# A two-layer transformer with a modulated second block: three modulation weight units loaded one up unit later

## The chip, the core and the metric

The kernel runs on one core of a Trainium2 chip. Five engines work from their own instruction streams: TensorE (matrix products, into the banks of PSUM), VectorE, ScalarE, GpSimd and SyncE, which here only issues loads from the memory of the chip (HBM) into SBUF, the on-chip memory of 128 partitions. Streams wait for one another with semaphores. The metric is the device time of one execution in microseconds (us); all tensors are 32-bit floats.

## The reference

Two blocks work on 256 tokens of 1024 features. The first has two layers, each a mixer (convolution, differential attention and memory attention side by side) and a feed-forward part; the second has one layer whose norms are scaled, shifted and gated by six vectors that are one product of a condition vector `c` with a 1024 x 6144 weight. The change touches the feed-forward part of the two layers and the place of that product:

```python
for l in range(2):                                   # first block
    x = layer_norm(ALPHA * x + hybrid_mixer(x, ...), ln1_g[l], ln1_b[l])
    ff = square(relu(x @ w_up[l])) @ w_down[l]        # 1024 -> 4096 -> 1024
    x = layer_norm(ALPHA * x + ff, ln2_g[l], ln2_b[l])
...
mod = silu(c) @ ada_w + ada_b                         # second block: 6 vectors of 1024
shift_m, scale_m, gate_m, shift_f, scale_f, gate_f = split(mod, 6)
```

## The kernel before

**Units.** Weights are read in units of 1024 x 512 (2 MB) into `ring`, three slots of SBUF in turn (`RING`, line 34). A layer has 30 units (`layer_units`, line 62): one for the memory, five for the mixer's input, two for its output, then the feed-forward part: eight of `w_up` and eight of `w_down`, called units 0 to 7 and 8 to 15 here, and six of `ada_w`, the modulation units 0 to 5. `ADA_UP` and `ADA_DOWN` (line 39) say behind which up and down units the modulation units lie, three and three in each layer. The whole modulation product, twelve units, is made in this way beside the feed-forward parts of the two layers. Everything else about the order follows from these two tuples: `ADA_AT` holds the positions of the modulation units in the order of loading, `ADA_POSITIONS` the steps in which they are worked on.

**SyncE** issues the loads in the order of the list. Before each it waits for its slot (`slot_free`, line 466): until TensorE is through with the unit three places earlier (seen at the first products of the unit behind it), or, if that was a modulation unit, until VectorE has summed it. A load whose slot is not free holds up all loads behind it.

**An up or down unit** is one step of Winograd's form of the 2 x 2 block product: seven products on TensorE instead of eight, in the order m1, m3, m2, m6, m5, m7, m4 (`seven`, line 2375; unit 0 opens with m1, m2, m4). m1, m2, m3 and m7 take blocks of the loaded weights; m5, m6 and m4 take sums of such blocks. VectorE makes these sums (`weight_sums`, line 1346): four operations on 128 x 1024 elements, of which m5 needs the first, m7 the second, m6 the third, m4 the fourth. They go by turns to tiles in `mid` and in `work`, so m6 of a unit reads in a row of the timeline as `acc<-ysq,mid` or `acc<-ysq,work`, m1 as the first `acc<-x,ring` of its unit. In step u, with TensorE on unit u, VectorE does, in this order:

```python
if u in ADA_POSITIONS:
    ada_sums(ADA_POSITIONS.index(u))        # L1572
if u + 1 < FFN_UNITS:
    weight_sums(u + 1)
if u - 2 in ADA_POSITIONS:
    ada_columns(ADA_POSITIONS.index(u - 2)) # L1576
...
    combine(u)                              # up units: the seven products put together
```

**A modulation unit** is not multiplied on TensorE. ScalarE scales its eight rows of blocks by silu(c) (`ada_scale`, line 898, eight operations), VectorE adds the eight to one row (`ada_sums`, line 1288, three operations of 2048, 1024 and 512 columns), TensorE turns the row into columns (`ada_turned`, four 128 x 128 turns, behind the unit after), and VectorE reduces these (`ada_columns`).

**ScalarE**, in step g, first makes the hidden group g - 1 from VectorE's combination (`hidden`: two relus at line 893, one square at 896), then copies the first bank of unit g (`first_bank`, line 887), then scales a modulation unit:

```python
hidden(g - 1)
first_bank(g)
if g + 1 in ADA_UP:
    ada_scale(ADA_UP.index(g + 1))
```

**GpSimd** makes the sums of tokens that the down units need, in quarters q: four operations on 128 x 512 elements (lines 582 to 587) as soon as the hidden groups 2q and 2q + 1 are there; quarters 2 and 3 wait besides until TensorE is through with units 9 and 11.

Of the kernel before, what the change touches and what calls it, by code (L numbers as in the profile page):

```python
# [35 lines left out]
UCOLS = 512  # L36
UROWS = 8
LAYER_UNITS = 30
ADA_UP, ADA_DOWN = (1, 3, 5), (0, 2, 4)
LAYER_ACCS = 20  # L40
HEAD_SIDE = (1, 0, 1)
OUT_BANKS = (2, 3, 0, 1)
# [3134 lines left out]
```

## Time and profile before

| what | value |
|---|---|
| median of 3 runs | 1304.3 us (1304.15 to 1304.51) |
| the profiled execution | 1303.27 us, of which the span from first to last instruction is 1301.3 |
| TensorE busy | 1287.2 us, 99% of the span |
| VectorE busy | 940.2 us, 72% |
| ScalarE busy | 423.2 us, 33% |
| GpSimd busy | 178.2 us, 14% |
| granted TensorE clock | 0.998 of full speed |
| feed-forward units, layer 0 and 1 | from 138 to 339 us, from 464 to 664 us |

The views name the engines PE (TensorE), DVE (VectorE), ACT (ScalarE), POOL (GpSimd) and SP (SyncE). A row of the timeline gives the start in us from the beginning of the span, the time to the end of the last of the operations that are merged in it, the engine, the line of the kernel, the operation, output<-inputs, shape and number; in square brackets, where the engine had been idle, the idle time and what ended it. Matmuls overlap one another a little, so the distance of two starts is the better measure of a product than its length. A releaser is the semaphore event that came last.

### The profile page before, as it was taken

The numbers are of one execution on the slowest core, as the hardware profiler recorded it, in microseconds if no ns is written. First come the engines' busy times: TensorE is split into PE (matmuls) and PEld (weight loads), VectorE is DVE, ScalarE is ACT, GpSimd is POOL, SyncE is SP. The second block draws the span as 40 slices with busy tenths as digits, with TensorE's granted clock in tenths as the row PEclk, the third lists the DMA queues.
The fourth block names the chain that finished last, engine by engine and source line by source line (L and its number), as shares of the span: only waits on it lengthen the run. The fifth ranks groups of instructions, "written<-read, shape, count | busy, mean of one in ns | idle before, by whom it ended". The sixth has DMA issues, their size and how long they took to land.

```text
span 1301.3 us, 34012 instructions
## 1 busy us (share of the span) xinstructions
PE 1287.2 (99%) x15139; PEld 1145.2 (88%) x15139; DVE 940.2 (72%) x1603; ACT 423.2 (33%) x920; POOL 178.2 (14%) x164
## 2 busy tenths in 40 slices
PE   9999999999999999999999999999999999999997
PEld 7975899988898589998877889999999986999986
DVE  4985798656698479867782789998997845765753
ACT  2254334311225433432144424555742103110101
POOL 3100322021000042203125010003100100011200
PEclk9999999999999999999999999999999999999999
DMA  9632567577443256757738797335645544654540
GB/s 330 200 130 97 195 226 284 199 267 256 142 151 130 98 195 231 283 201 266 249 93 231 179 251 205 131 131 185 207 131 196 191 168 130 196 170 157 179 178 33
DMA packets 132930, 243.17 MB, mean 187 GB/s; under 512 B 7237, under 2 KB 37725, under 8 KB 132273
## 3 DMA queue, kind: packets, MB, share of 16 engines
q1 hardware_dynamic: 122506, 218.00, 48.7%
q0 software_dynamic: 9872, 22.80, 7.2%
q8 instruction: 120, 1.97, 0.6%
q10 hardware_dynamic: 407, 0.20, 0.1%
q14 instruction: 25, 0.20, 0.0%
HBM read 231.49 MB, written 6.34 MB: 183 GB/s over the span
## 4 chain that ended last, share of the span: by engine, by line
PE 88%; DVE 7%; DMA 2%; issue 1%; ACT 1%; POOL 1%; SPq 0%; DVEq 0%
PE acc L2214 55%; PE scr L2214 17%; PE pvw L2214 9%; DVE mid L1523 2%; PE scr L2824 1%; PE scr L2319 1%; DMA ring<-in_w_mem_kv 1%; PE ptb L2214 1%; PE ptb L2328 1%; DMA ring<-in_w_up 1%; PE pvw L2338 1%; PE pvw L2858 1%; PE ptb L2658 0%; DMA strip_rows<-hid 0%; DVE hid L1882 0%
## 5 line engine op out<-in xcount | busy, mean ns | idle before, releaser
L2214 PE MATMUL acc<-y,ring 128*64 128x128 f32 (+1 forms) x2048 | 154.1, 283 | 0.0
L2214 PEld LDWEIGHTS acc<-y,ring 128*64 128x64 f32 (+1 forms) x2048 | 139.3, 142 | 8.5 <-issue 2.3
L2214 PE MATMUL acc<-ring,big 128*128 128x256 f32 (+1 forms) x376 | 115.6, 454 | 0.0
L2214 PEld LDWEIGHTS acc<-ring,big 128*128 128x128 f32 x376 | 70.6, 190 | 33.4 <-issue 27.0
L2214 PE MATMUL acc<-ring,hid 128*128 128x256 f32 (+1 forms) x364 | 99.1, 417 | 0.0
L2214 PE MATMUL acc<-x,ring 128*64 128x128 f32 (+1 forms) x1472 | 98.9, 278 | 0.0
L2214 PEld LDWEIGHTS acc<-x,ring 128*64 128x64 f32 (+1 forms) x1472 | 89.6, 139 | 4.7 <-issue 3.2
L903 ACT ACTIVATE ring<-ring,silc 128x512 f32<-128x512 f32 x96 | 60.1, 709 | 93.8 <-DMA ring<-in_ada_w 93.8
L2214 PEld LDWEIGHTS acc<-ring,hid 128*128 128x128 f32 x364 | 68.4, 190 | 22.2 <-issue 14.9
L2214 PE MATMUL acc<-ysq,ring 128*64 128x128 f32 x1184 | 71.2, 273 | 0.0
L1295 DVE TENSOR_TENSOR ring<-ring 128x2048 f32<-128x2048 f32 (+1 forms) x24 | 44.2, 1843 | 33.7 <-ACT ring L903 33.2
L2214 PE MATMUL scr<-ysq,ring 128*64 128x128 f32 x1120 | 67.5, 273 | 0.0
L2214 PEld LDWEIGHTS acc<-ysq,ring 128*64 128x64 f32 x1184 | 66.4, 137 | 0.0
L2214 PEld LDWEIGHTS scr<-ysq,ring 128*64 128x64 f32 x1120 | 62.8, 137 | 0.0
L1523 DVE SCALAR_TENSOR_TENSOR mid<-upad,pc,mid 128x256 f32<-128x256 f32 x120 | 48.7, 476 | 0.0
L728 ACT ACTIVATE work<-work,nm 128x256 f32<-128x256 f32 x80 | 39.6, 496 | 25.8 <-DVE nm L1269 15.6
L1146 ACT ACTIVATE big<-acc 128x512 f32<-128x512 f32 x19 | 11.3, 596 | 109.7 <-PE acc L2214 109.7
L1354 DVE TENSOR_TENSOR mid<-ring 128x1024 f32<-128x1024 f32 x16 | 19.5, 1221 | 36.7 <-DMA ring<-in_w_down 24.2
L1355 DVE TENSOR_TENSOR ring<-ring 128x1024 f32<-128x1024 f32 x32 | 45.4, 1420 | 0.0
L582 POOL TENSOR_TENSOR big<-hid 128x512 f32<-128x512 f32 x8 | 15.1, 1884 | 212.6 <-PE pvw L2214 150.4
L2214 PE MATMUL acc<-mid,ring 128*64 128x128 f32 x704 | 41.0, 273 | 0.0
L893 ACT ACTIVATE hid<-big 128x512 f32<-128x512 f32 x16 | 10.1, 629 | 90.7 <-DVE pt L1399 90.6
(592 smaller groups left out, 2771.8 us busy)
## 6 DMA issues: line engine op xcount, KB each, us to landing
ring<-in_w_in SPq DMA_DIRECT2D x24, 2048.0 KB, 10.9
ring<-in_w_up SPq DMA_DIRECT2D x16, 2048.0 KB, 8.7
ring<-in_w_down SPq DMA_DIRECT2D x16, 2048.0 KB, 7.9
ring<-in_ada_w SPq DMA_DIRECT2D x12, 2048.0 KB, 12.9
ring<-in_w_ffn_in SPq DMA_DIRECT2D x22, 1024.0 KB, 7.1
ring<-in_w_out SPq DMA_DIRECT2D x6, 2048.0 KB, 7.9
ring<-in_w_o_ssd SPq DMA_DIRECT2D x4, 2048.0 KB, 8.5
ring<-in_w_ffn_out SPq DMA_DIRECT2D x4, 2048.0 KB, 8.3
```

The source lines that it names most:

```text
L582: pool.tensor_tensor(s1, a21, a22, ALU.add).then_inc(sh_ready, 1)
L728: ins = act.activation(pr[:, i % 2, j, :], lg[:, i % 2, j, :], ACT.Exp, scale=-1.0, bias=nm[:, i % 2, j:j + 1], accum_out=zz[:, i % 2, j:j ...
L903: act.activation(ring[:, n % RING, k, :], ring[:, n % RING, k, :], ACT.Copy, scale=silc[:, 1, k:k + 1]).then_inc(ada_scaled, 1)
L1295: steps.link(tt(w[:, 0:width, :], w[:, 0:width, :], w[:, width:2 * width, :], ALU.add))
L1354: tt(t[:, 0], b12, b11, ALU.subtract).then_inc(t_ready, 1)
L1355: tt(b12, b22, b12, ALU.subtract).then_inc(t_ready, 1)
L1523: ins = stt(cy[:, c, :], upad[:, c, tap:tap + T], w, cy[:, c, :], ALU.mult, ALU.add)
L2214: ins = pe.matmul(dst, w, m, start=start, stop=stop, is_transpose=turned, skip_group_check=True)
L2319: ins = pe.matmul(scr[m][:, t, :], q[half, t * P:(t + 1) * P], keys[half, h, :], start=True, stop=True)
L2328: ins = pe.transpose(ptb[:, 2 * j + kt, :], at[:, i % 2, j, kt * P:(kt + 1) * P], ident[:, :])
L2338: ins = pe.matmul(pvb[:, 0, :], vt[:, h * P:(h + 1) * P], pt[:, i % 2, kt, :], start=kt == 0, stop=kt == TT - 1)
L2824: ins = pe.matmul(scr[i % 2][:, m, :], q2[:, 2 * j + m, t * P:(t + 1) * P], kvn[:, :], start=True, stop=True)
```

## The change

One tuple of three numbers changes:

```diff
--- before.py
+++ after.py
@@ -36,7 +36,7 @@
 UCOLS = 512
 UROWS = 8
 LAYER_UNITS = 30
-ADA_UP, ADA_DOWN = (1, 3, 5), (0, 2, 4)
+ADA_UP, ADA_DOWN = (2, 4, 6), (0, 2, 4)
 LAYER_ACCS = 20
 HEAD_SIDE = (1, 0, 1)
 OUT_BANKS = (2, 3, 0, 1)
```

The first three modulation units of each layer are loaded behind up units 2, 4 and 6 instead of 1, 3 and 5, and what is done with them moves one step on each engine. On SyncE, at the beginning and at the end of the up units of a layer (`ring<-in_w_up` an up unit, `in_ada_w` a modulation unit, `in_w_out` the mixer's output, `in_w_down` a down unit):

```order
 L482 DMA ring<-in_w_out 128x8x512 x2
-L482 DMA ring<-in_w_up 128x8x512 x2
+L482 DMA ring<-in_w_up 128x8x512 x3
 L482 DMA ring<-in_ada_w 128x8x512
 L482 DMA ring<-in_w_up 128x8x512 x2
```

```order
 L482 DMA ring<-in_ada_w 128x8x512
-L482 DMA ring<-in_w_up 128x8x512 x2
+L482 DMA ring<-in_w_up 128x8x512
 L482 DMA ring<-in_w_down 128x8x512
 L482 DMA ring<-in_ada_w 128x8x512
```

Three up units come before the first modulation unit, and one instead of two lies between the third modulation unit and the first down unit. The slots change with the places: modulation units 0, 1 and 2 followed one another in the slot that the mixer's last unit left, and it went on to the first down unit; now they follow one another in the slot that unit 0 leaves, which goes on to modulation unit 3, and the first down unit takes the slot of unit 6.

On VectorE, from the end of combination 1 (line 1399) on; lines 1295 and 1296 are a modulation sum, lines 1354 to 1359 the weight sums of one unit, the combination follows at line 1388. Before:

```order
L1399 TENSOR_TENSOR pt<-big,pvw 128x256
L1354 TENSOR_TENSOR work<-ring 128x1024
L1355 TENSOR_TENSOR ring<-ring 128x4x256
L1357 TENSOR_TENSOR work<-ring,work 128x1024
L1359 TENSOR_TENSOR work<-ring,work 128x1024
L1388 TENSOR_TENSOR big<-pt,acc 128x512
```

Now:

```order
L1399 TENSOR_TENSOR pt<-big,pvw 128x256
L1295 TENSOR_TENSOR ring<-ring 128x2048
L1295 TENSOR_TENSOR ring<-ring 128x1024
L1296 TENSOR_TENSOR pre<-ring 128x512
L1354 TENSOR_TENSOR work<-ring 128x1024
L1355 TENSOR_TENSOR ring<-ring 128x4x256
L1357 TENSOR_TENSOR work<-ring,work 128x1024
L1359 TENSOR_TENSOR work<-ring,work 128x1024
L1388 TENSOR_TENSOR big<-pt,acc 128x512
```

The modulation sum 0 has moved from step 1 to step 2, where it stands ahead of the weight sums of unit 3; steps 4 and 6 get the next two in the same way, and steps 1, 3 and 5 lose theirs.

On ScalarE, at the beginning of the up units (line 887 the copy of a first bank, 903 the scaling, 893 and 896 a hidden group):

```order
 L887 ACTIVATE pt<-acc 128x512
+L893 ACTIVATE hid<-big 128x4x128
+L893 ACTIVATE hid<-pt 128x4x128
+L896 ACTIVATE hid<-hid 128x1024
+L887 ACTIVATE pt<-acc 128x512
 L903 ACTIVATE ring<-ring,silc 128x512 x8
```

The first scaling stands behind hidden group 0 and the bank of unit 1, and so ahead of hidden group 1; it used to stand ahead of hidden group 0.

## Rows read from the trace of the kernel before

**Rows 1.** Page, part 4: the chain that ended last, by engine.

```profile
PE 88%; DVE 7%; DMA 2%; issue 1%; ACT 1%; POOL 1%; SPq 0%; DVEq 0%
```

**Rows 2.** Timeline, unit 2: start us, us, engine, operation [idle before].

```profile
164.76 1.95 PE L2214 MATMUL acc<-x,ring 128*64 128x128 f32 x32
...
168.25 1.95 PE L2214 MATMUL acc<-x,ring 128*64 128x128 f32 x32
170.49 1.97 PE L2214 MATMUL acc<-ysq,mid 128*64 128x128 f32 x32 [0.29 <-DVE mid L1357]
...
495.45 1.95 PE L2214 MATMUL acc<-ysq,mid 128*64 128x128 f32 x32
...
165.03 0.58 ACT L887 ACTIVATE pt<-acc 128x512 f32<-128x512 f32 x1
```

**Rows 3.** Timeline, TensorE: first products of units 4 to 6, m6 of 5.

```profile
190.49 1.92 PE L2214 MATMUL acc<-x,ring 128*64 128x128 f32 x32
...
203.41 1.97 PE L2214 MATMUL acc<-x,ring 128*64 128x128 f32 x32
...
208.70 1.92 PE L2214 MATMUL acc<-ysq,work 128*64 128x128 f32 x32
...
215.68 1.92 PE L2214 MATMUL acc<-x,ring 128*64 128x128 f32 x32
```

**Rows 4.** Timeline, ScalarE and SyncE's queue: scalings 1 and 2, unit 6's load.

```profile
179.27 5.01 ACT L903 ACTIVATE ring<-ring,silc 128x512 f32<-128x512 f32 x8 [2.37 <-DMA ring<-in_ada_w]
...
205.29 5.01 ACT L903 ACTIVATE ring<-ring,silc 128x512 f32<-128x512 f32 x8 [6.17 <-DMA ring<-in_ada_w]
...
203.87 12.59 SPq L482 DMA_DIRECT2D ring<-in_w_up  x2
```

**Rows 5.** Timeline, VectorE, layer 0: modulation sum 0, weight sums, combination 1.

```profile
162.76 3.54 DVE L1295 TENSOR_TENSOR ring<-ring 128x2048 f32<-128x2048 f32 x2
...
166.95 1.22 DVE L1354 TENSOR_TENSOR mid<-ring 128x1024 f32<-128x1024 f32 x1
...
169.22 1.22 DVE L1357 TENSOR_TENSOR mid<-ring,mid 128x1024 f32<-128x1024 f32 x1
...
171.61 0.68 DVE L1388 TENSOR_TENSOR big<-pt,acc 128x512 f32<-128x512 f32 x1
...
174.05 1.22 DVE L1354 TENSOR_TENSOR work<-ring 128x1024 f32<-128x1024 f32 x1
```

**Rows 6.** Timeline, three engines: quarter 1's sums, layer 0; modulation sum 4, layer 1.

```profile
196.40 0.63 ACT L893 ACTIVATE hid<-big 128x512 f32<-128x512 f32 x1 [9.50 <-DVE pt L1399]
...
198.72 1.27 POOL L582 TENSOR_TENSOR big<-hid 128x512 f32<-128x512 f32 x1 [15.16 <-ACT hid L896]
...
201.16 2.29 DVE L1355 TENSOR_TENSOR ring<-ring 128x1024 f32<-128x1024 f32 x1
...
203.38 2.29 DVE L1357 TENSOR_TENSOR work<-ring,work 128x1024 f32<-128x1024 f32 x1
...
597.09 4.50 DVE L1295 TENSOR_TENSOR ring<-ring 128x2048 f32<-128x2048 f32 x2 [2.44 <-ACT ring L903]
...
597.09 3.41 POOL L587 TENSOR_TENSOR big<-hid,big 128x512 f32<-128x512 f32 x1
```

**Rows 7.** Timeline, TensorE and VectorE, units 7 to 9; page, part 6: two loads.

```profile
228.60 1.97 PE L2214 MATMUL acc<-x,ring 128*64 128x128 f32 x32
...
240.97 1.99 PE L2214 MATMUL acc<-ring,hid 128*128 128x256 f32 x8
...
258.34 1.89 PE L2214 MATMUL acc<-work,big 128*128 128x256 f32 x8
...
248.78 3.55 DVE L1295 TENSOR_TENSOR ring<-ring 128x2048 f32<-128x2048 f32 x2 [7.27 <-ACT ring L903]
...
ring<-in_w_up SPq DMA_DIRECT2D x16, 2048.0 KB, 8.7
ring<-in_w_down SPq DMA_DIRECT2D x16, 2048.0 KB, 7.9
```
## The prediction

> **What bounds the kernel now.** I read the chain of waits first: 88% of the chain that ends last is TensorE's own work [rows 1]. So I went to the one stretch that the change touches, the sixteen feed-forward units of each layer, and read TensorE's timeline there for gaps. In layer 0 there is one that belongs to the change: unit 2's product m6 starts at 170.49, although m2, begun at 168.25, should have let it go 1.75 us later, at 170.00. It lost 0.49 us to VectorE's third weight sum [rows 2]. Layer 1 has no such wait at this place; its m6 at 495.45 shows no idle time [rows 2]. Elsewhere the units follow one another without a gap: unit 4 with its turning 12.92 us (190.49 to 203.41), unit 5 12.27 (203.41 to 215.68) [rows 3]. So the change cannot gain more than about half a microsecond in all, and the question is whether it makes new waits. The place to look is always the same: m6 of a unit needs the third weight sum of that unit, and VectorE makes that sum one step ahead.
>
> **The change, part by part.** It adds and removes nothing. Three loads, three scalings on ScalarE, three modulation sums on VectorE and three turnings on TensorE move by one unit step, from the odd steps 1, 3, 5 to the even steps 2, 4, 6. The turnings cost TensorE the same wherever they stand, so their net is zero.
>
> The gain: in step 1 VectorE no longer sums a modulation unit before unit 2's weights. That sum takes 4.19 us (162.76 to 166.95) [rows 5], far more than the 0.49 us that m6 waited, so this wait goes: **-0.49 us**, in layer 0 alone. Unit 2's weights are now the second load of the layer's start instead of the modulation unit, and have some 24 us until they are summed at 162.8; that costs nothing.
>
> The cost at units 3 and 5: in the new order VectorE sums a modulation unit in steps 2 and 4. There, as before, ScalarE finishes hidden groups 1 and 3, and these are what GpSimd waits for to make the token sums of quarters 0 and 1: four operations, which start when ScalarE's squaring ends (196.40 to 198.72, 2.3 us after the relu begins) [rows 6]. Before, they fell on steps with nothing but the weight sums. One such GpSimd operation between two of VectorE's moves the next VectorE operation from 1.14 us (half of 166.95 to 169.22) [rows 5] to 2.22 (201.16 to 203.38) [rows 6]: 1.08 us each, **4.3 us for four**.
>
> For unit 5 I count from the first product of unit 3. That product gives back unit 2's slot; unit 4's weights are requested, and modulation unit 1 right behind them. The same pair of loads needed 14.51 us (164.76 to 179.27) and 14.80 (190.49 to 205.29) from such a product to the start of the scaling [rows 2, 4]; I take 14.65. Scaling 5.0, about 0.1 to VectorE [rows 4], modulation sum 4.19, third weight sum 3.49 (166.95 to 169.22 + 1.22) [rows 5]: 27.45. GpSimd's first request comes 2.3 us after the scaling's end, when VectorE has done one of its three modulation operations, so all four of its operations come in before the third weight sum: 27.45 + 4.3 = 31.8. TensorE is there after 12.92 + 12.27 + 5.24 (unit 3 with the turning behind it, unit 4, and three products as from 164.76 to 170.00) = 30.4 [rows 2, 3]. m6 of unit 5 waits **1.4 us**; the two loads' spread makes that 1.2 to 1.6. Without GpSimd in between it would have 3.0 us to spare.
>
> For unit 3 in layer 0: ScalarE's copy at 165.03 ends at 165.6 [rows 2], the scaling at 170.6, and with 4.19 + 3.49 + 4.3 the third sum is there at 182.6. TensorE, 0.49 us earlier, arrives at 170.00 + 12.25 = 182.2 [rows 2, 3]: a wait of 0.4. But such a wait lies behind unit 3's first product, which starts the clock of unit 5's count, so unit 5 then waits as much less. The pair costs 1.4 us in either layer, however it is split.
>
> At units 3 and 5, the other things that m5 to m4 ask for follow the third sum by at most 1.14 + 0.6 + 2.44 us (fourth sum, the column reduction, the combination: 171.61 to 174.05 [rows 5]; the reduction is an estimate of half an operation), and m4 starts three products, 5.2 us, after m6, so one wait covers all. SyncE's queue: unit 6's weights go out at unit 5's first product as before, and modulation unit 2 behind them, since its slot is free when modulation sum 1 ends, about then.
>
> The cost at the border to the down projection: the slot of the first down unit was modulation unit 2's, free early; it is now unit 6's, free when unit 7 starts. So the load goes out some 0.5 us after unit 7's first product (203.41 to 203.87) [rows 3, 4] and lands 7.9 later [rows 7]. Weight sums 4.66, combination of unit 7 2.44 [rows 5]: 15.5 us after unit 7's start, where before the combination ended with TensorE at 241.5, 12.9 after 228.60 (248.78 less its 7.27 of idle time) [rows 7]. From there it is 7.27 us to modulation sum 3 [rows 7], then 4.19 + 3.49: 30.4. TensorE needs 12.92 for unit 7 and its turning [rows 3] and 17.37 from unit 8's start to m6 of unit 9 (240.97 to 258.34) [rows 7]: 30.3. So what was 1.9 us to spare is used up: **0.1 us** a layer, between 0 and, if the load takes the 8.7 us of an up unit [rows 7], 0.9. Behind unit 9 the loads are tied to TensorE as before, and the order does not change.
>
> **Sum.** Layer 0: -0.49 + 1.4 + 0.1 = +1.0. Layer 1: +1.4 + 0.1 = +1.5. Together +2.5 us. The profiled execution took 1303.27 us, 1301.3 of it the span; the sum makes it 1305.8. It lies 1.0 under the median of the runs, 1304.3, so the median should become **1306.8**.
>
> **A rule against the count.** First the rows on two engines at one port: the pair of modulation operations that took 3.54 us alone [rows 5] took 4.50 beside GpSimd, and GpSimd's operation of 1.27 took 3.41 [rows 6]. They do not run at half speed each; one stands still for the other's whole instruction. The Trainium skill (SBUF — State Buffer, section SBUF: two separate sides) says the same, an exclusive lock that goes to whichever instruction starts first; it says nothing of turns. Read to the letter, VectorE's next instruction, which is ready when the last one ends, could keep GpSimd out until the chain is done, and the cost at units 3 and 5 would be none: that is the first rival below. The trace disagrees so far: the operations at 201.16 and 203.38 alternate with GpSimd's [rows 6].
>
> **The rivals.**
> 1. GpSimd stays behind. If no more than two of its four operations come in before the third weight sum, 27.45 + 2.2 = 29.6 is under 30.4 and units 3 and 5 do not wait: -0.49 + 0.2 = -0.3, so 1304.0, not slower. Point from which it decides: three of four. For it: the modulation operations are longer (2.2 us) than the weight sums that were seen alternating. Against it: that one GpSimd operation did get in between two modulation operations at 597.09 [rows 6]. Chance 0.13. A mixed case, one layer or half of the operations, gives +0.5 to +1.7, so 1304.8 to 1306.0: 0.12.
> 2. The first down unit lands late. With the 8.7 us of an up unit unit 9 waits 0.9 us in each layer: +1.6 more, 1308.4. For it: another load is requested right behind it. Against: 7.9 is the median of sixteen, and several of those had one behind too. Chance 0.13.
> 3. The change does nothing that can be seen: out of the question for the order, which is fixed in the code, and for the time it is the case where gain and cost cancel, contained in the first rival.
>
> **How the numbers follow.** The forecast, 1306.8 with its own range of 1306.2 to 1307.6 (0.2 us either way for the loads in each layer, up to 0.2 for unit 9), has 0.62. What a measurement of this kernel can tell from no change is about 0.2%, 2.6 us, and the forecast's +2.5 stands right at this bound; I put 0.30 of its 0.62 above it and 0.32 below. Slower: 0.30 + 0.13 = 0.43. Same: 0.32 + 0.13 + 0.12 less a little for the unforeseen = 0.55. Faster by more than 2.6 us: there is only half a microsecond to be had, 0.02. The range leaves out the first rival and a little of the second: 1304.7 to 1308.6.
>
> **What would show it.** In the changed kernel's TensorE timeline: no idle time before m6 of unit 2; in layer 0 some 0.4 before m6 of unit 3 and 1.0 before m6 of unit 5, in layer 1 together 1.4, each ended by VectorE's third weight sum (the write to the sum tile from ring and itself); about 0.1 before m6 of unit 9. On VectorE, in steps 2 and 4, the modulation operations and the first weight sums longer by 1.1 us each, with four GpSimd operations of over 2 us between them. The first weight sum of unit 8 waits for the down load. I am wrong if GpSimd's four operations lie behind the third weight sum, if the modulation load lands later than 15 us after the unit's first product, or if a wait stands at another product.

## The result and the profile after

The changed kernel takes **1308.34 us** (median of 6 runs, 1307.73 to 1310.71) against 1304.22 (1303.39 to 1304.61): a ratio of 1.0033, 95% interval 1.0023 to 1.0043. It is 4.1 us slower (0.33%), inside the range of the prediction, 1.5 us above its forecast, and past the 0.2% that it took for what a measurement can tell. The profiled execution took 1307.84 us with a span of 1305.9, 4.6 more than before. The granted clock is 0.999 for 0.998.

The page's chain that ended last, by engine (part 4), of the changed kernel; before it read PE 88%, DMA 2% [rows 1]:

```profile
PE 81%; DVE 9%; DMA 5%; ACT 3%; issue 1%; POOL 1%; SPq 0%; DVEq 0%
```

TensorE's waits in the changed kernel (what it waited for: us in total, times, longest), over the whole span:

```profile
PE acc L2214 <- DVE work L1357: 4.9, 4, 1.8
```

So the chain now leaves TensorE for loads, ScalarE and VectorE, and comes back at four products m6, each time at the third weight sum (line 1357). The wait of unit 2 [rows 2] is gone, four others have come. The next rows are TensorE's in the changed kernel. First, in layer 0, m6 of unit 2 and the first product of unit 3; then, for either layer, m2 and m6 of unit 5 and m2 and m6 of unit 9, in layer 0 with unit 9's first product (254.25) ahead of them:

```profile
169.93 1.95 PE L2214 MATMUL acc<-ysq,mid 128*64 128x128 f32 x32
...
176.92 1.95 PE L2214 MATMUL acc<-x,ring 128*64 128x128 f32 x32
...
205.63 1.92 PE L2214 MATMUL acc<-x,ring 128*64 128x128 f32 x32
209.34 1.97 PE L2214 MATMUL acc<-ysq,work 128*64 128x128 f32 x32 [1.79 <-DVE work L1357]
...
254.25 1.89 PE L2214 MATMUL acc<-ring,hid 128*128 128x256 f32 x8
...
257.70 1.89 PE L2214 MATMUL acc<-ring,hid 128*128 128x256 f32 x8
259.97 1.99 PE L2214 MATMUL acc<-work,big 128*128 128x256 f32 x8 [0.38 <-DVE work L1357]
...
532.88 1.92 PE L2214 MATMUL acc<-x,ring 128*64 128x128 f32 x32
...
536.01 1.97 PE L2214 MATMUL acc<-ysq,work 128*64 128x128 f32 x32 [1.21 <-DVE work L1357]
...
584.37 1.89 PE L2214 MATMUL acc<-ring,hid 128*128 128x256 f32 x8
587.76 1.99 PE L2214 MATMUL acc<-work,big 128*128 128x256 f32 x8 [1.50 <-DVE work L1357]
```

In layer 0, m6 of unit 5 starts 3.71 us after the product before it, where undisturbed products follow at 1.75 (1.73 in the down units). I call the difference, 1.96, the wait; the bracket shows some 0.17 less because matmuls overlap. By this count the four waits are 1.96 and 0.54 in layer 0, 1.38 and 1.66 in layer 1, together 5.5. Less the 0.49 of unit 2, and less 0.42 that TensorE lost in the profile of before at m4 of unit 1 and by chance not here (below), that is 4.6, as much as the spans differ.

That the two agree so well is in part chance, because three smaller terms nearly cancel. TensorE came to the feed-forward part of layer 0 0.38 us later (138.35 for 137.97). A product behind a wait takes 0.05 to 0.1 longer to its successor. And the turning that now stands behind unit 7 costs less than the one that stood behind unit 6. From unit 7's first product to unit 9's it is 24.91 us with that turning (229.34 to 254.25) and was 24.57 without (228.60 [rows 7] to 253.16), so it costs 0.34. Between two up units a turning costs 0.65 (12.92 against 12.27 [rows 3]). That is some 0.3 less in each layer. Unit 9's first product in the kernel before:

```profile
253.16 1.89 PE L2214 MATMUL acc<-ring,hid 128*128 128x256 f32 x8
```

Behind the wait at unit 5, layer 0, stand these rows of ScalarE, VectorE and GpSimd (changed kernel, timeline): scaling 1; modulation sum 1 and the first three weight sums of unit 5; quarter 1's token sums.

```profile
192.42 5.01 ACT L903 ACTIVATE ring<-ring,silc 128x512 f32<-128x512 f32 x8 [5.13 <-DMA ring<-in_ada_w]
...
197.53 4.51 DVE L1295 TENSOR_TENSOR ring<-ring 128x2048 f32<-128x2048 f32 x2 [3.12 <-ACT ring L903]
202.08 1.65 DVE L1296 TENSOR_TENSOR pre<-ring 128x512 f32<-128x512 f32 x1
203.65 2.29 DVE L1354 TENSOR_TENSOR work<-ring 128x1024 f32<-128x1024 f32 x1
205.86 2.29 DVE L1355 TENSOR_TENSOR ring<-ring 128x1024 f32<-128x1024 f32 x1
208.07 1.21 DVE L1357 TENSOR_TENSOR work<-ring,work 128x1024 f32<-128x1024 f32 x1
...
199.64 1.32 POOL L582 TENSOR_TENSOR big<-hid 128x512 f32<-128x512 f32 x1 [21.02 <-ACT hid L896]
201.04 2.14 POOL L584 TENSOR_TENSOR hid<-hid 128x512 f32<-128x512 f32 x1
203.14 1.72 POOL L585 TENSOR_TENSOR big<-big,hid 128x512 f32<-128x512 f32 x1
204.94 2.13 POOL L587 TENSOR_TENSOR big<-hid,big 128x512 f32<-128x512 f32 x1
```

The two engines take turns: from the second of the two modulation operations merged at 197.53 on, each VectorE operation is long while a GpSimd operation lies in it (the first two weight sums take 2.29 us), and the third sum, begun after GpSimd's end at 207.07, is short again (1.21). All four GpSimd operations came in before it. The third sum ends at 209.28, m6 starts at 209.34.

Behind the wait at unit 9 stand the first product of unit 7, the request of the first down unit on SyncE, and unit 8's first weight sum on VectorE, in layer 0 and then in layer 1 (changed kernel, timeline):

```profile
229.34 1.92 PE L2214 MATMUL acc<-x,ring 128*64 128x128 f32 x32
...
229.75 0.37 SPq L482 DMA_DIRECT2D ring<-in_w_down  x1
...
237.76 1.23 DVE L1354 TENSOR_TENSOR mid<-ring 128x1024 f32<-128x1024 f32 x1 [3.51 <-DMA ring<-in_w_down]
...
556.01 1.92 PE L2214 MATMUL acc<-x,ring 128*64 128x128 f32 x32
...
556.42 0.37 SPq L482 DMA_DIRECT2D ring<-in_w_down  x1
...
565.55 1.23 DVE L1354 TENSOR_TENSOR mid<-ring 128x1024 f32<-128x1024 f32 x1 [4.21 <-DMA ring<-in_w_down]
```

From request to sum it is 8.0 us in layer 0 and 9.1 in layer 1, where the prediction had 7.9 [rows 7] for both.

### The profile page after: what moved, and what is told of

Its sections match the earlier page's. It is cut to its first block, busy times and chain, and to the rows that moved or that the text cites. A ratio compares the mean times of both kernels' runs of the same rounds, so it can differ in the third digit from the quotient of the medians.

```text
span 1305.9 us, 34012 instructions
## 1 busy us (share of the span) xinstructions
PE 1286.4 (99%) x15139; PEld 1144.7 (88%) x15139; DVE 942.7 (72%) x1603; ACT 422.9 (32%) x920; POOL 178.0 (14%) x164
## 4 chain that ended last, share of the span: by engine, by line
PE 81%; DVE 9%; DMA 5%; ACT 3%; issue 1%; POOL 1%; SPq 0%; DVEq 0%
PE acc L2214 51%; PE scr L2214 15%; PE pvw L2214 8%; DMA ring<-in_ada_w 2%; DVE mid L1523 2%; ACT ring L903 2%; DMA ring<-in_w_down 1%; DVE ring L1295 1%; PE scr L2824 1%; DMA ring<-in_w_mem_kv 1%; PE scr L2319 1%; PE ptb L2214 1%; DVE ring L1355 1%; PE ptb L2328 1%; PE pvw L2338 1%
## 5 line engine op out<-in xcount | busy, mean ns | idle before, releaser
L1295 DVE TENSOR_TENSOR ring<-ring 128x2048 f32<-128x2048 f32 (+1 forms) x24 | 48.2, 2008 | 42.8 <-ACT ring L903 42.4
```

The costliest lines, as they stand in the source:

```text
L1295: steps.link(tt(w[:, 0:width, :], w[:, 0:width, :], w[:, width:2 * width, :], ALU.add))
```

## The experiments

One table for all runs: waits in us as counted above, layer 0 / layer 1. "m6, 3+5" is units 3 and 5 together. "Scaling 1" is its start after unit 3's first product, "sum 8" the start of unit 8's weight sums after unit 7's first product.

| kernel | median us | ratio to before, 95% | m4, 1 | m6, 2 | scaling 1 | m6, 3+5 | sum 8 | m6, 9 |
|---|---|---|---|---|---|---|---|---|
| before | 1304.2 to 1304.7 | | 0.42 / 0 | 0.49 / 0 | | 0 / 0 | | 0 / 0 |
| changed | 1308.34 | 1.0033, 1.0023 to 1.0043 | 0 / 0 | 0 / 0 | 15.50 / 14.92 | 1.96 / 1.38 | 8.42 / 9.54 | 0.54 / 1.66 |
| e4, changed again | 1308.31 | 1.0039, 1.0028 to 1.0050 | 0.40 / 0.39 | 0 / 0 | 14.66 / 14.59 | 1.08 / 1.03 | 8.22 / 9.50 | 0.34 / 1.62 |
| e11, changed again | 1308.25 | 1.0028, 1.0016 to 1.0040 | 0.38 / 0.38 | 0 / 0 | 14.46 / 14.71 | 0.87 / 1.14 | 8.72 / 9.50 | 0.84 / 1.61 |
| e1 | 1305.33 | 1.0008, 1.0000 to 1.0017 | 0.40 / 0.38 | 0 / 0 | 15.14 / 15.13 | 0 / 0 | 8.37 / 9.57 | 0.49 / 1.69 |
| e2 | 1306.36 | 1.0015, 1.0006 to 1.0024 | 0.40 / 0.40 | 0 / 0 | 14.87 / 15.99 | 1.30 / 2.40 | 8.41 / 9.55 | 0 / 0 |
| e3 | 1302.93 | 0.9987, 0.9979 to 0.9996 | 0.41 / 0.39 | 0 / 0 | 14.87 / 14.99 | 0 / 0 | 8.34 / 9.49 | 0 / 0 |
| e5 | 1306.10 | 1.0011, 1.0003 to 1.0020 | 0.40 / 0.41 | 0.49 / 0.49 | 8.94 / 9.68 | 0 / 0 | 8.25 / 9.79 | 0.36 / 1.91 |
| e7 | 1305.63 | 1.0011, 1.0002 to 1.0020 | 0.39 / 0.40 | 0 / 0 | 12.16 / 12.46 | 0.18 / 0.17 | 8.44 / 9.31 | 0.54 / 1.41 |
| e8 | 1308.07 (one run) | | 0.40 / 0.40 | 0 / 0 | 15.35 / 14.67 | 1.77 / 1.09 | 8.45 / 9.60 | 0.55 / 1.71 |
| e9 | 1302.09 | 0.9981, 0.9972 to 0.9990 | 0 / 0 | 0 / 0 | 14.62 / 14.93 | 0 / 0 | 8.34 / 9.56 | 0 / 0 |
| e10 | 1302.86 | 0.9987, 0.9978 to 0.9996 | 0 / 0 | 0.14 / 0 | | 0 / 0 | | 0 / 0 |

**GpSimd's quarters 0 and 1 later (e1).** The changed kernel, with quarters 0 and 1 held back until VectorE has made the weight sums of the step:

```diff
                     if q >= 2:
                         pool.wait_ge(t_free, (DOWN_UNITS - 2) * l + 2 * (q - 2) + 2)
+                    else:
+                        pool.wait_ge(t_ready, 4 * (FFN_UNITS * l + 2 * q + 3) + 4)
```

> The changed kernel, in which GpSimd's token sums of quarters 0 and 1 wait besides until VectorE has made the weight sums of units 3 and 5, so that they fall on steps 3 and 5 without a modulation sum. Theory (GpSimd's four operations lengthen VectorE's chain in step 4): no idle time before m6 of unit 5 in either layer, VectorE's modulation sum and three weight sums take 7.7 us there and not 11.7; the waits before m6 of unit 9 stay, 0.1 to 1.7 us a layer. Of the 4.1 us over the kernel before about 3.3 go: 1305 to 1306. Rival (the loads alone are late, GpSimd hides in time that VectorE has anyway): 1.4 to 2.0 us before m6 of unit 5 stay, about 1308.

Measured: 1305.33, 3.0 less than the changed kernel. The same stretch of layer 0 in e1's timeline, VectorE's modulation sum 1 and unit 5's third weight sum, then GpSimd's first operation and m6 of unit 5:

```profile
197.55 3.55 DVE L1297 TENSOR_TENSOR ring<-ring 128x2048 f32<-128x2048 f32 x2 [3.17 <-ACT ring L905]
...
204.01 1.22 DVE L1359 TENSOR_TENSOR work<-ring,work 128x1024 f32<-128x1024 f32 x1
...
206.64 1.28 POOL L584 TENSOR_TENSOR big<-hid 128x512 f32<-128x512 f32 x1 [21.24 <-DVE work L1361]
...
207.75 1.92 PE L2216 MATMUL acc<-ysq,work 128*64 128x128 f32 x32
```

From the start of the modulation sum to the end of the third weight sum VectorE now needs 7.68 us instead of 11.75: 4.07 for four operations, 1.02 each. The load came as late as in the changed kernel (scaling 1 at 15.1), and m6 does not wait; it has 2.5 us to spare. So GpSimd's four operations are a cause at units 3 and 5: without them this load is early enough. Unit 9 waits as before, 0.49 and 1.69, which keeps the two causes apart.

**The border: unit 9's sums ahead of modulation sum 3 (e2), both (e3).** In step 8 VectorE makes unit 9's weight sums first. e3 is e1 and e2 together.

```diff
-                    if u in ADA_POSITIONS:
+                    if u in ADA_POSITIONS and u != 8:
                         ada_sums(ADA_POSITIONS.index(u))
                     if u + 1 < FFN_UNITS:
                         weight_sums(u + 1)
+                    if u == 8:
+                        ada_sums(ADA_POSITIONS.index(u))
```

> The changed kernel with VectorE's order turned round in step 8 alone: the weight sums of unit 9 ahead of modulation sum 3. Theory (unit 9 waits for the row: late load of the first down unit, combination 7, hidden group 7, scaling 3, modulation sum 3, weight sums): no idle time before m6 of unit 9, the waits before m6 of unit 5 stay at 1.2 to 2.0 us a layer; 1306 to 1307. Rival (unit 9 waits for its own weights, whose load is late): the waits before m6 of unit 9 stay at 0.5 to 1.7 us, 1308.3.

> Both edits of the two kernels before: GpSimd's quarters 0 and 1 behind the weight sums of units 3 and 5, and in step 8 the weight sums of unit 9 ahead of modulation sum 3. Theory: all four waits gone, and with them unit 2's of the kernel before: 1303.3 to 1304.2, not slower than the kernel before, by up to 0.9 us faster. Rival (the cost lies in the loads and shows at other products): 1306 or more, with idle time before other products of units 3 to 12.

Measured: e2 1306.36, 2.0 less than the changed kernel; e3 1302.93, 5.4 less. The two nearly add up (3.0 + 2.0). In e2 TensorE's waits on the third sum, layer 0 (138 to 290 us) and layer 1 (462 to 610), are those of unit 5 alone (a wait of 0.17 at unit 3, which the table counts in, is too short for this view):

```profile
PE acc L2216 <- DVE work L1357: 1.0, 1, 1.0
...
PE acc L2216 <- DVE work L1357: 2.1, 1, 2.1
```

Unit 8's sums start as late as before the edit (9.55 in layer 1); what went is the modulation sum in the chain between them and unit 9's. e3 has none of the waits that the change brought and lies 1.6 under the kernel before, also 0.4 under the lowest time that I expected: I had not counted the cheaper turnings (some 0.6 us in the two layers), nor the waits at units 1 and 2 that the kernel before may have in both layers (below).

**The changed kernel again (e4, e11).** Both are the changed kernel with nothing altered.

> The changed kernel once more, beside the others on the same chip, to see which of its waits differ from one execution to the next: 1307.5 to 1310. If the sizes of the waits hang on when the loads land, the waits before m6 of unit 5 lie between 1.0 and 2.0 us and those before m6 of unit 9 between 0.1 and 1.7, not as in the first profile, and each goes up and down with its load by the same amount. If the first profile's 0.5 in layer 0 and 1.7 in layer 1 belong to the layers (layer 1 has more work on VectorE), they come again.

> The changed kernel a third time, beside the kernel above on one chip: 1307.5 to 1309, 0.8 to 1.8 us before m6 of units 3 and 5 together in each layer, each the start of scaling 1 after unit 3's first product less 13.56 us to within 0.05; 0.3 to 0.6 before m6 of unit 9 in layer 0 and 1.4 to 1.9 in layer 1.

Measured: 1308.31 and 1308.25. What differs from profile to profile is the landing of modulation unit 1: scaling 1 starts 14.46 to 15.50 us after unit 3's first product in the six layers of the three profiles of this kernel, and the wait at units 3 and 5 goes with it, 0.87 to 1.96. In every layer of these three profiles, e2 and e8 the wait at units 3 and 5 is the scaling's start less 13.56, to within 0.03. At unit 9 the same rule holds with 7.88. Unit 9's waits are 0.34 to 0.84 in layer 0, where e11 went past the 0.6 that I expected, and 1.61 to 1.66 in layer 1. That layer 1's are longer came again each time; it belongs to the layer.

**The first modulation unit as before (e5).** One third of the change undone.

```diff
-ADA_UP, ADA_DOWN = (2, 4, 6), (0, 2, 4)
+ADA_UP, ADA_DOWN = (1, 4, 6), (0, 2, 4)
```

> Modulation units behind up units 1, 4 and 6: the first as in the kernel before, the second and third as in the changed one. Modulation unit 1 is then the only load that goes out at unit 3's first product, since unit 4's weights find their slot free early. Theory (m6 of unit 5 waits as long after unit 3's first product as the modulation load takes, less 13.6 us): scaling 1 starts some 9 to 10 us after that product instead of 14.6 to 16.0, and no wait is left at unit 5, although VectorE's modulation sum still stands in step 4 with GpSimd's four operations between; the waits at unit 9 stay at 0.3 to 0.5 in layer 0 and 1.6 to 1.7 in layer 1, unit 2's 0.5 may come back: 1305.5 to 1306.8. Rival (the sum in step 4 is what costs, wherever its load stands): 0.7 us or more stay at unit 5, over 1307.

Measured: 1306.10. Unit 2 waits 0.49 again, now in both layers. Modulation unit 1 no longer follows another load that was held up by unit 3's start; it is requested by itself, and scaling 1 starts at 8.94 and 9.68. SyncE's request and ScalarE's scaling 1 in e5, layer 0:

```profile
178.44 0.37 SPq L482 DMA_DIRECT2D ring<-in_ada_w  x1
...
186.91 5.01 ACT L903 ACTIVATE ring<-ring,silc 128x512 f32<-128x512 f32 x8 [1.60 <-DMA ring<-in_ada_w]
```

GpSimd's operations are still there (VectorE's stretch takes 12.02 and 11.76 us), and nothing waits at units 3 and 5. The border keeps its 0.36 and 1.91, the second 0.2 more than I expected. So GpSimd costs nothing at unit 5 where scaling 1 starts well ahead of the 13.56; here the load did so because it was not the second of a pair behind one freed slot.

**Half of modulation unit 1 (e7).** Only four of its eight blocks are loaded, so what is scaled and summed of it is in part old data; the second block's modulation vectors are not the reference's.

```diff
+                if n == ADA_AT[1]:
+                    kn, src = 4, src[:, 0:4 * P, :]
```

> The changed kernel, but of modulation unit 1 of each layer only the first half (512 of 1024 rows) is loaded; the other half is what lay in the slot. Theory: with half the bytes the load lands 2 to 3 us earlier, scaling 1 starts 12 to 13 us after unit 3's first product, below the 13.6 from which m6 of unit 5 waits, so its wait goes with GpSimd's operations where they are; unit 9's waits stay (0.3 to 0.5 and 1.6): 1305 to 1306. Rival (the load has time to spare): m6 of unit 5 waits 0.8 us or more, 1308.

Measured: 1305.63, 2.7 less than the changed kernel. Scaling 1 starts at 12.16 and 12.46, VectorE's stretch takes 11.76 and 11.75 us with GpSimd's operations in it, and unit 5 does not wait; 0.18 and 0.17 stay at unit 3, whose modulation unit was not halved. The second cause of the wait, the landing, is shown with that: either the earlier landing or GpSimd's absence takes it away.

**The first down load from the other layer's weights (e8).** In layer 0 unit 8 is loaded from layer 1's weights and the other way round, so the down product is another one than the reference's. The question was whether the 1.1 us by which this load is later in layer 1 belongs to the weights' place in HBM.

```diff
-                src = whole[l:l + 1, k0 * P:(k0 + kn) * P, c0:c0 + cn]
+                ls = 1 - l if n == FFN_AT[UP_UNITS] else l
+                src = whole[ls:ls + 1, k0 * P:(k0 + kn) * P, c0:c0 + cn]
```

> The changed kernel, in which the first down unit of each layer is read from the other layer's weights, so the output is not the reference's. In four executions the weight sums of unit 8 began 8.2 to 8.4 us after unit 7's first product in layer 0 and 9.5 in layer 1, and unit 9 waited 0.3 to 0.5 and 1.6 to 1.7. If the extra 1.1 us belongs to where these weights lie in HBM, the two change places: 9.5 in layer 0, 8.3 in layer 1, and the waits with them. If it belongs to the place in the program (what else runs in layer 1), they stay.

Measured: it does not. e8's request on SyncE and unit 8's first weight sum on VectorE, layer 0 and layer 1:

```profile
229.76 0.37 SPq L483 DMA_DIRECT2D ring<-in_w_down  x1
...
237.79 1.23 DVE L1355 TENSOR_TENSOR mid<-ring 128x1024 f32<-128x1024 f32 x1 [3.50 <-DMA ring<-in_w_down]
...
556.60 0.37 SPq L483 DMA_DIRECT2D ring<-in_w_down  x1
...
565.79 1.23 DVE L1355 TENSOR_TENSOR mid<-ring 128x1024 f32<-128x1024 f32 x1 [4.14 <-DMA ring<-in_w_down]
```

8.0 and 9.2 us: layer 1's is late wherever it reads. What makes it late stays open.

**The half microsecond at unit 1 (e9, e10).** In the table m4 of unit 1 waits 0.4 in most kernels, not in the first profile of the changed one, and in the kernel before in layer 0 alone. At the start of the feed-forward part VectorE's weight sums of unit 1 and GpSimd's four operations on tokens (lines 570 and 573) become ready at nearly the same time. These are the rows of the kernel before and of the changed one. Before, layer 0, VectorE's first two sums and GpSimd's first operations, then layer 1, the first sum and GpSimd's first operations:

```profile
147.09 3.40 DVE L1354 TENSOR_TENSOR work<-ring 128x1024 f32<-128x1024 f32 x1 [0.18 <-DMA ring<-in_w_up]
150.41 3.38 DVE L1355 TENSOR_TENSOR ring<-ring 128x1024 f32<-128x1024 f32 x1
...
147.05 5.65 POOL L570 TENSOR_TENSOR y<-y,hid 128x1024 f32<-128x1024 f32 x2 [33.01 <-DVE ysq L1371]
...
472.94 1.23 DVE L1354 TENSOR_TENSOR work<-ring 128x1024 f32<-128x1024 f32 x1
...
472.95 6.74 POOL L570 TENSOR_TENSOR y<-y,hid 128x1024 f32<-128x1024 f32 x2 [33.95 <-DVE ysq L1371]
```

Changed, layer 0:

```profile
147.39 1.23 DVE L1354 TENSOR_TENSOR work<-ring 128x1024 f32<-128x1024 f32 x1
148.53 3.38 DVE L1355 TENSOR_TENSOR ring<-ring 128x1024 f32<-128x1024 f32 x1
...
147.42 6.71 POOL L570 TENSOR_TENSOR y<-y,hid 128x1024 f32<-128x1024 f32 x2 [33.00 <-DVE ysq L1371]
```

GpSimd was 0.04 us ahead in layer 0 before, and all four of VectorE's sums took 3.3 to 3.4; it was 0.01 behind in layer 1 and 0.03 behind in the changed kernel, and the first took 1.23. That is the 0.42. Who is first goes with the load of unit 1. In the ten profiles in which no edit orders the two, GpSimd was ahead in 17 layers, and there VectorE's first sum had waited for that load (0.18 to 0.85 us of idle time); in the three layers where it was behind, the sum had not.

The wait of unit 2 hangs on this too. Where the modulation sum stands in step 1, m6 of unit 2 waits 0.49 if GpSimd was ahead at unit 1 (before in layer 0, e5 in both layers) and not at all if it was behind (before in layer 1). In e4 and e11 GpSimd was ahead, the modulation sum had moved, and unit 2 doesn't wait. So it takes both. In e10 (the kernel before with one line) and e9 (e3 with the same line) GpSimd lets VectorE's four sums go first:

```diff
                 pool.wait_ge(sx_ready, 4 * (l + 1))
+                pool.wait_ge(t_ready, 4 * (FFN_UNITS * l + 1) + 4)
```

> The kernel with both edits (GpSimd's quarters 0 and 1 behind the weight sums of units 3 and 5; in step 8 the weight sums of unit 9 ahead of modulation sum 3), and besides GpSimd's four operations of the first norm's gain and offset behind the weight sums of unit 1, which they made 11 to 13 us long instead of 4.7. Theory: the 0.4 us before m4 of unit 1 goes in both layers too, and no wait of the units 1 to 9 is left: 0.8 us less than with both edits, about 1302.1. Rival: the four operations of 2.2 us now lie between VectorE's weight sums of unit 2, and m6 of unit 2 or m4 of unit 1 waits as long: 1303 or more.

> The kernel before, with its modulation units where they were, and only GpSimd's four operations of the first norm's gain and offset put behind the weight sums of unit 1. It tells whether the fastest version so far, 1302.1, owes anything to the moved modulation units. Theory (the units 1 to 9 need no wait in either order, and all that was to be gained are the waits of the kernel before: 0.4 before m4 of unit 1, 0.5 before m6 of unit 2): no idle time left at units 1 to 9, 1302.1 to 1303.4, the same as the version with the moved units and three edits. Rival (the moved units give something of their own once their waits are mended): 1303.6 or more, with idle time before m6 of unit 2.

Measured: e10 1302.86, 1.8 less than before; e9 **1302.09** (1301.89 to 1302.47), the fastest here, 0.19% under the kernel before and 6.2 us under the changed one. Of TensorE's waits in e9's units only one is left, in layer 0 as in layer 1, at the opening products (the waits view):

```profile
PE pvw L2219 <- DVE x L1326: 0.2, 1, 0.2
```

The chain of e9 by engine, to be held against [rows 1]:

```profile
PE 91%; DVE 5%; DMA 1%; ACT 1%; POOL 1%; issue 1%; SPq 0%; DVEq 0%
```

The later modulation units are worth a little once their waits are gone. The medians of e9 and e10 differ by 0.8 us, with intervals that overlap and on different chips, so they don't settle it; the profiles do. From unit 0's first product to unit 15's last, e9 takes 198.09 us in either layer, e10 198.60 and 198.44: 0.86 in all, of which 0.14 is e10's wait at unit 2 and some 0.3 in each layer the cheaper turning. So of the two theories for e10 neither was quite right: its time came as expected, with 0.14 left before m6 of unit 2, and the moved units do give something of their own.

Of e10's gain of 1.8 the trace shows 0.42 at unit 1 and 0.35 at unit 2 (0.49 to 0.14) against the profile of before; that profile was itself 1.0 under the median of its runs. A likely reason is that GpSimd was ahead at unit 1 in only one of its layers. In the eight other profiles in which it was ahead at all, it was so in both, and a second layer would lose 0.42 and 0.49 more: 0.9 of the 1.0, and with it 1.7 of e10's 1.8. This is an estimate; no second profile of the kernel before shows it.

## Why the prediction was right or wrong

**Unit 2, -0.49: right in size, with half of its cause.** m6 follows m2 at 1.75 (168.18 to 169.93) in the changed kernel, and e5 brings 0.49 back by itself. But the modulation sum in step 1 makes this wait only where GpSimd was ahead at unit 1, which I had not seen. "In layer 0 alone" was how that one execution fell, and the first profile of the changed kernel, in which GpSimd was behind, could not have tested the term; e4 and e11 do.

**GpSimd between the modulation sum and the weight sums: right.** All four operations came in ahead of the third weight sum in both layers of all three profiles of the changed kernel, so the first rival, that GpSimd stays behind, is out; e1 shows that without them there is no wait. Two of the four took over 2 us, as expected of all (2.14 and 2.13; the others 1.32 and 1.72). They cost 4.07 us instead of 4.3, and VectorE's stretch took 11.75 instead of the 11.98 of the sum (4.19 + 3.49 + 4.3). One side stands still for an instruction of the other, as with the lock of the Trainium skill (SBUF — State Buffer, section SBUF: two separate sides), and the trace agrees so far: a weight sum that takes 1.21 us by itself takes 2.29. Who gets the port next the section doesn't say; in these rows the sides alternate one by one, so the reading by which VectorE keeps GpSimd out is not borne out.

**Units 3 and 5, +1.4 a layer: the step is right, its size scatters.** With the scaling 14.65 after unit 3's first product, the measured rule gives 14.65 - 13.56 = 1.1 (my own terms give 1.3 before rounding, and 0.2 less with GpSimd's measured price). The landing, which I took from two pairs of loads 0.3 apart, was 14.46 to 15.50. The 15.50, in layer 0 of the first profile, is past the 15 that I had named as a sign of being wrong; only the landing moved, and the wait followed it as the count says. So the pair of layers cost 3.34, 2.11 and 2.01 in the three profiles of the changed kernel, 2.5 in the mean, for 2.8 predicted. The stated split in layer 0, 0.4 at unit 3 and 1.0 at unit 5, was 0 and 1.96 in the first profile and 0.17 and 0.91, 0.17 and 0.70 in the others. In the first profile VectorE was through with unit 1's sums 1.9 us earlier than before (VectorE was first at the port, above), and with it hidden group 0 and scaling 0 (164.00, for the 165.6 that I had); in e4 scaling 0 starts at 165.53, and unit 3 waits 0.17.

**Unit 9, +0.1 a layer: the term that was mis-sized.** It cost 0.54, 0.34 and 0.84 in layer 0 and 1.66, 1.62 and 1.61 in layer 1: 2.0 to 2.5 in all, for 0.2. In layer 0 the load was right (8.0 for 7.9); the two sides of my difference, 30.4 against 30.3, were each off by 0.2 in the wrong direction, TensorE's side because I took the turning behind unit 7 for as dear as one between up units: the third sum lets m6 start 30.63 us after unit 7's first product (259.97 - 229.34), and TensorE would be there 0.54 earlier, after 30.09. In layer 1 the load took 9.1, later than the 8.7 of the second rival. So this rival's mechanism came true in one layer of the two, with 1.6 for its 0.9, and I had given it 0.13. Why the load is later there stays open (e8). The fault was to take a median of sixteen loads [rows 7] for one certain load with no cover left, where the spread of that one load was what mattered; a difference of two sums of thirty microseconds was also not good to a tenth.

**The turnings, put at nothing.** They do not cost the same wherever they stand: the third of each layer costs 0.34 behind unit 7 and cost 0.65 behind unit 6, a gain of some 0.3 a layer that the prediction left out.

**The sum.** -0.49 + 2.8 + 0.2 = +2.5 was predicted. -0.49 + 3.3 + 2.2 - 0.42 = +4.6 is the measured sum of the waits in the first profile; with the mean of three profiles at units 3 and 5 (2.5) it is the border, 2.0 too small, that makes most of the miss. That the forecast still came within 1.5 us of the median is in part luck, since terms that it did not have (the turnings, unit 1, and what lies ahead of the feed-forward part) pull both ways. The 0.42 at m4 of unit 1 stood in the profile of before, and I passed over it: I looked for gaps that the change makes or closes, not for those that fall out differently from one execution to the next.

**Slower or same.** The forecast stood at the bound of 0.2%. I leaned to no visible change (0.55 against 0.43), and the time fell on the slower side.

## What to carry to other kernels

Before moving a step of one engine, list what the other engines do at the new place by the event that starts them, not by the code: the modulation sums were moved to the very steps in which GpSimd wakes up and shares VectorE's port, and a 4 us overlap cost nothing until a late load had used up the slack. Price a load that has lost its cover by the spread of such loads at its place, not by their median. Where two engines fight for a port, holding back the one that nobody waits for (one wait on a semaphore) paid here, while the change itself cost time: 3.0 us for the two quarters in the changed kernel, and 1.8 for lines 570 and 573 in the kernel before.

## What was not expected of the hardware

- The first down load takes 1.1 us longer in layer 1 than in layer 0, in all ten profiles in which it waits for unit 6's slot (0.8 to 1.5), and it keeps its place in the program when the source is exchanged. While it is under way the core's DMA engines move as much per second in both layers. The DMA view of the changed kernel, from the request to the first weight sum (229.75 to 237.80 us and 556.40 to 565.60), layer 0 and layer 1:

```profile
DMA packets 1240, 2.52 MB, mean 313 GB/s; under 512 B 16, under 2 KB 16, under 8 KB 1239
...
DMA packets 1422, 2.89 MB, mean 315 GB/s; under 512 B 16, under 2 KB 16, under 8 KB 1421
```

  The load itself is 2.10 MB, and the one load requested behind it is the only other of its size in that time. So by this count some 0.4 MB of the load behind it had moved by the time it was whole in layer 0, and 0.8 in layer 1: the next load was worked on while a part of the first was still missing. Why more so in layer 1 stays open.
- The run time of the changed kernel scatters: nine runs of e4 lie between 1306.9 and 1313.7, those of e9, in which no product of the units waits for a load, within 0.6 us. That the loads make the difference is not shown; six runs of e11, the same kernel as e4, lie within 1.3.
- At unit 1 GpSimd's start, 0.04 us ahead of VectorE's or 0.01 to 0.04 behind it, decides over some 2.2 us of one weight sum (3.40 or 1.23) and 0.4 us of TensorE's time in that layer, with the modulation sum in step 1 another 0.49.
